# A chunked RWKV-7 scan: triangular inverse on 64 partitions, two 64-row product stages in one, and the scan's transfers merged and reordered

## The reference

```python
def step(state, inp):
    r_t, w_t, k_t, v_t, kk_t, a_t = inp
    sa = einsum('zbhvk,zbhk->zbhv', state, -kk_t)
    state = (state * w_t[..., None, :] + sa[..., :, None] * (kk_t * a_t)[..., None, :]
             + v_t[..., :, None] * k_t[..., None, :])
    y = einsum('zbhvk,zbhk->zbhv', state, r_t)
    return state, y
```

## Time and profile before

| | us |
|---|---|
| median of 3 runs (3359.9 to 3370.8) | 3364.0 |
| the profiled execution | 3362.9 |
| its span, first to last instruction | 3361.1 |

### The profile page before, as it was taken

One profiled execution on the slowest core, in us unless ns is written; L12 is line 12 of the kernel. 1 busy time (PEld: TensorE's weight loads), 2 busy tenths in 40 slices (PEclk: granted clock), 3 DMA queues, 4 the chain that ended last, 5 costly groups with the idle time before them and its releaser, 6 DMA issues.

```text
span 3361.1 us, 42103 instructions
## 1 busy us (share of the span) xinstructions
PE 3258.0 (97%) x15943; PEld 2692.0 (80%) x15943; DVE 1852.6 (55%) x2360; ACT 1310.0 (39%) x2139; POOL 1580.3 (47%) x1492
## 2 busy tenths in 40 slices
PE   7999999999889999999899999999999999999998
PEld 6788887777578888888588878888888888888886
DVE  3666565666667676772531034455455455455556
ACT  4544345554255665662442232223233233223222
POOL 4544443334278888885564443323323323323323
PEclk9999999999899999999899999999999999999999
DMA  5444454443455555552633323323323323323323
GB/s 171 122 151 138 141 154 132 129 120 103 114 137 143 129 130 141 146 135 82 242 115 136 113 69 113 107 88 107 112 83 109 111 81 117 103 84 117 107 82 106
DMA packets 666051, 405.06 MB, mean 121 GB/s; under 512 B 193534, under 2 KB 597178, under 8 KB 665338
## 3 DMA queue, kind: packets, MB, share of 16 engines
q1 hardware_dynamic: 665850, 402.38, 41.1%
HBM read 347.05 MB, written 54.53 MB: 119 GB/s over the span
## 4 chain that ended last, share of the span: by engine, by line
PE 50%; DVE 1%; ACT 0%; issue 0%; POOL 0%; DMA 0%; SPq 0%; DVEq 0%; ACTq 0%; POOLq 0%
PE f_bank L2207 9%; PE f_bank L2209 9%; PE f_bank L2208 9%; PE f_bank L2245 4%; PE f_bank L2247 4%; PE f_bank L2246 4%; PE f_bank L2185 2%; PE f_bank L2186 2%; PE f_bank L2187 2%; PE f_bank L2128 1%; PE f_bank L2129 1%; PE f_bank L2130 1%; PE f_bank L2163 0%; DMA orw_plain<-oat 0%; DVE orw_plain L2701 0%
## 5 line engine op out<-in xcount | busy, mean ns | idle before, releaser
L2496 POOL TENSOR_TENSOR w_lo_b<-w_raw_b,w_hi_b 128x1024 fp32r<-128x1024 f32 x176 | 435.9, 2479 | 903.4 <-ACT w_hi_b L2372 898.1
L2207 PE MATMUL f_bank<-act_rounded,w_lo_b 128*128 128x512 f32 x1408 | 549.2, 390 | 1.2 <-DVE act_rounded L2608 1.2
L2209 PE MATMUL f_bank<-act_rounded,w_hi_b 128*128 128x512 f32 x1408 | 547.8, 389 | 0.0
L2208 PE MATMUL f_bank<-act_rounded,w_hi_b 128*128 128x512 f32 x1408 | 547.8, 389 | 0.0
L1295 POOL TENSOR_TENSOR ring_w_rounded<-ring_w_plain,ring_w_hi 128x1024 fp32r<-128x1024 f32 x134 | 330.3, 2470 | 427.5 <-ACT ring_w_hi L1311 427.5
L1635 PE MATMUL slab_ps<-h_hi,ring_w_rounded 128*128 128x512 f32 x1056 | 426.4, 404 | 2.8 <-DVE h_lo L1462 2.4
L1636 PE MATMUL slab_ps<-h_lo,ring_w_hi 128*128 128x512 f32 x1056 | 414.9, 393 | 0.0
L1637 PE MATMUL slab_ps<-h_hi,ring_w_hi 128*128 128x512 f32 x1056 | 414.2, 392 | 0.0
L2372 ACT CAST w_hi_b<-w_raw_b 128x1024 fp32r<-128x1024 f32 x176 | 185.1, 1053 | 449.6 <-DMA w_raw_b<-in_w_ffn_up_dram 203.9
L2207 PEld LDWEIGHTS f_bank<-act_rounded,w_lo_b 128*128 128x128 f32 x1408 | 264.5, 188 | 55.7 <-DVE act_rounded L2608 1.1
L2209 PEld LDWEIGHTS f_bank<-act_rounded,w_hi_b 128*128 128x128 f32 x1408 | 264.3, 188 | 55.2
(11 more groups left out here) (434 smaller groups left out, 6176.9 us busy)
## 6 DMA issues: line engine op xcount, KB each, us to landing
ring_w_plain<-in_w_in_dram SPq DMA_DIRECT2D x190, 512.0 KB, 4.1
w_raw_b<-in_w_ffn_gate_dram SPq DMA_DIRECT2D x88, 512.0 KB, 3.6
w_raw_b<-in_w_ffn_up_dram SPq DMA_DIRECT2D x88, 512.0 KB, 3.6
w_raw_b<-in_w_ffn_down_dram SPq DMA_DIRECT2D x42, 512.0 KB, 3.9
w_raw_b<-in_w_out_dram SPq DMA_DIRECT2D x16, 1024.0 KB, 5.0
zt<-slab_out SPq DMA_DIRECT2D x63, 256.0 KB, 4.3
hid_plain<-in_w_ffn_down_dram SPq DMA_DIRECT2D x21, 512.0 KB, 4.2
oa_plain<-in_w_ffn_down_dram SPq DMA_DIRECT2D x21, 512.0 KB, 3.8
```

The costliest lines, as they stand in the source:

```text
L2207: pe.matmul(o, wl[:, k, :], act_hi[:, kk, :], start=kk == 0, stop=False)
L2208: pe.matmul(o, wh[:, k, :], act_lo[:, kk, :], start=False, stop=False)
L2209: return pe.matmul(o, wh[:, k, :], act_hi[:, kk, :], start=False, stop=stop)
L2496: pool.tensor_tensor(low(r), slab_raw(j % 2), high(r).bitcast(F32), ALU.subtract).then_inc(slab_low, 1)
```

## The change

- **Inverse (GpSimd).** Each matrix is now on two partitions, which hold the columns of one parity: 64 partitions with 32 matrices. 31 steps in place of 30, on at most 144 elements a partition in place of 240. The result is a tensor of its own, `inv`, cleared before each inverse; so the rows and columns of the matrices are put in an order of their own (even tokens first within a half, and for the backward direction the halves exchanged), which VectorE's masks (`mask_ba`, `mask_br`, `mask_ka`, made at the start) and the operands' order follow.
- **Products of b and k (TensorE).** The stages ab and ak become one, abk: 8 products of 64 rows, straight from `bk` and `var`, alternating between the two halves of the array's rows and between two banks. ScalarE's stage bd with its four copies goes. The masked results are taken by VectorE in three stages (n, ab, ak) with operations on 64 partitions, 8 in place of 5.
- **Transfers (SyncE).** The six loads of a unit become two, the five of the bonus two, since `zt` has its rows in another order. In odd slots the wait for the inverse, its store and the transfers into `d_bd` and `low` for one unit come before the loads of the next matrices; the other unit's transfers move to the start of the even slot.

```diff
-PE_SLOT = (("x1", "u"), ("ab", "v"), ("lx", "u"), ("ak", "v"), ("x3", "u"), ("av", "v"), ("qg", "u"),
+PE_SLOT = (("x1", "u"), ("abk", "v"), ("lx", "u"), ("x3", "u"), ("av", "v"), ("qg", "u"),
            ("bk", "v"), ("yh", "u"), ("akv", "v"), ("ts", "u"))
-GATE_SHARE = {"ab": 2, "ak": 2, "av": 3, "bk": 3, "akv": 3, "ts": 3}
-DVE_SLOT = (("ab", "v"), ("xadd", "u"), ("ak", "v"), ("decays", "w"), ("qg", "u"), ("operands", "w"), ("state", "u"))
+GATE_SHARE = {"abk": 2, "lx": 3, "av": 2, "bk": 3, "akv": 3, "ts": 3}
+DVE_SLOT = (("n", "v"), ("xadd", "u"), ("ab", "v"), ("ak", "v"), ("decays", "w"), ("qg", "u"), ("operands", "w"), ("state", "u"))
...
-                    for j in range(HALF - 2, 0, -1):
-                        n = HALF - 1 - j
-                        shape = [HALF, j, n]
-                        st = step[:, 0:j * n].rearrange("p (i t) -> p i t", t=n)
-                        pool.tensor_tensor(st, m[:, 0:j, j:j + 1].broadcast_to(shape), m[:, j:j + 1, j + 1:HALF].broadcast_to(shape),
-                                           ALU.mult).then_inc(inv_chain, 1)
+                    rows = lambda t: t.rearrange("p (r c) n -> p r c n", r=2)
+                    for j in range(HALF - 1, 0, -1):
+                        k, n, c, at = (j + 1) // 2, EVERY - j // 2, j // 2, (j % 2) * EVERY + j // 2
+                        shape = [CH, 2, k, n]
+                        st = step[:, 0:2 * k * n].rearrange("p (r i n) -> p r i n", r=2, n=n)
+                        pool.tensor_tensor(st, rows(m)[:, :, 0:k, at:at + 1].broadcast_to(shape),
+                                           x[:, at:at + 1, c:EVERY].unsqueeze(1).broadcast_to(shape), ALU.mult).then_inc(inv_chain, 1)
                         pool.wait_ge(inv_chain, done + 1)
-                        pool.tensor_tensor(m[:, 0:j, j + 1:HALF], m[:, 0:j, j + 1:HALF], st, ALU.add).then_inc(inv_chain, 1)
+                        pool.tensor_tensor(rows(x)[:, :, 0:k, c:EVERY], rows(x)[:, :, 0:k, c:EVERY], st, ALU.add).then_inc(inv_chain, 1)
...
+                    if slot % 2 == 0 and slot >= 0:
+                        blocks_back(slot + 1)
+                    paired = slot % 2 and 0 <= slot + 1 < NUNIT
+                    if paired:
+                        it = (slot + 1) // 2
+                        sp.wait_ge(inverted, it + 1)
+                        for r in range(2):
+                            sp.dma_start(yb[it % 2, :, :, r, :], inv[it % 2][r * HALF:(r + 1) * HALF, :, :]).then_inc(inv_stored[it % 2], 16)
                     if 0 <= v < NUNIT:
-                        it, s = divmod(v, 2)
-                        sp.wait_ge(taken_dve, DVE_AT["ab", v])
+                        sp.wait_ge(taken_dve, DVE_AT["n", v])
+                        sp.dma_start(nb[(v // 2) % 4, v % 2].rearrange("q p t -> p q t"), n_sb[:, :, :]).then_inc(n_stored, 16)
+                    if paired:
+                        sp.wait_ge(inv_stored[it % 2], 32 * (it // 2 + 1))
+                        blocks_back(slot + 1)
+                    if 0 <= v < NUNIT and v % 2:
+                        it = v // 2
+                        sp.wait_ge(n_stored, 16 * (v + 1))
+                        if it >= 2:
+                            sp.wait_ge(inverted, it - 1)
+                        src = nb[it % 4].rearrange("z q (e i) t -> (z q e) i t", e=2)
+                        for hb in range(2):
+                            for r in range(2):
+                                at = r * HALF + 16 * hb
+                                sp.dma_start(blocks[it % 2][at:at + 16, :, :],
+                                             src[:, hb * HALF:(hb + 1) * HALF, hb * HALF:(hb + 1) * HALF]).then_inc(n_landed[it % 2], 16)
...
-                    elif name == "ab":
-                        pe.wait_ge(taken_act, ACT_AT["bd", n])
+                    elif name == "abk":
+                        pe.wait_ge(taken_dve, DVE_AT["operands", n])
+                        if n >= 1:
+                            pe.wait_ge(taken_act, ACT_AT["akv", n - 1])
                         for q in Q:
-                            ins = pe.matmul(bank[1][:, q, :], b_bd[:, q, :], xar[st][:, q, CH:3 * CH], start=True, stop=True)
+                            for e in range(2):
+                                r = slice(CH * e, CH * e + CH)
+                                ins = pe.matmul(bank[1 + 2 * e][:, q, :], bk[r, q, :], var[r, q, CH:3 * CH], start=True, stop=True)
...
-                            dve.scalar_tensor_tensor(out=t[:, :, CH:P], in0=ordered(kk_in, s), scalar=-1.0, in1=by_scan(e_ex, s),
-                                                     op0=ALU.mult, op1=ALU.mult).then_inc(prep_ready, 1)
-                            dve.tensor_tensor(t[:, :, P:3 * CH], ordered(r_in, s), by_scan(e_in, s), ALU.mult)
...
-                            dve.tensor_copy(av[:, :, 0:CH], t[:, :, CH:P]).then_inc(taken_dve, 1)
+                            for r in range(2):
+                                dve.tensor_tensor(placed(var[:, :, CH:P], r), half(kk_in, back_in, r), half(e_ex, back_e, r), ALU.mult)
+                            dve.tensor_tensor(var[:, :, P:3 * CH], ordered(r_in, s), by_scan(e_in, s), ALU.mult)
+                            dve.tensor_tensor(xar[st][:, :, P:3 * CH], ordered(r_in, s), by_scan(e_in, s), ALU.mult)
```

More of the change, by code:

```diff
@@ L56 @@
 HALF = 32
+EVERY = HALF // 2
 PARAMS = {}
@@ L459, in store_gate, with blocks_back @@
                         sp.dma_start(zt[row:row + P, :], gate[c % 2][:, :]).then_inc(gate_stored[c % 2], 16)
-                def bonus_rows(b, row):
-                    return zt[row + (b // 2) * P:row + (b // 2 + 1) * P, (b % 2) * HS:(b % 2 + 1) * HS]
+                def blocks_back(n):
+                    it, s = divmod(n, 2)
+                    if n >= 2:
+                        sp.wait_ge(made, PE_AT["x3", n - 2])
+                    else:
+                        sp.wait_ge(zeroed, N_ZERO)
+                    for hb in range(2):
+                        first = 8 * (2 * hb + s)
+                        src = yb[it % 2].rearrange("b i r t -> b i (r t)")[first:first + 8].rearrange("(q e) i t -> e i q t", e=2)
+                        for e in range(2):
+                            at = CH * e + HALF * hb
+                            sp.dma_start(d_bd[s][at:at + HALF, :, at:at + HALF], src[e]).then_inc(d_landed[s], 16)
+                    for e in range(2):
+                        first, last = CH * e + HALF * s, CH * e + HALF * (1 - s)
+                        sp.dma_start(low[s][first:first + HALF, :, last:last + HALF],
+                                     nb[it % 4, s, :, first:first + HALF, last - CH * e:last - CH * e + HALF].rearrange("q i t -> i q t")
+                                     ).then_inc(d_landed[s], 16)
                 load(0)
@@ L643, in _, with in_turn @@
                 dve.wait_ge(zeroed, N_ZERO)
-                strict = g.order[:, 0:1, :].broadcast_to([P, NQ, CH])
-                within = g.order[:, 1:2, :].broadcast_to([P, NQ, CH])
+                each = lambda t: t[:, :].unsqueeze(1).broadcast_to([P, NQ, CH])
+                mask_ba, mask_br, mask_ka = ([each(t) for t in m] for m in masks)
+                mask_kr = each(g.order[:, 1, :])
+                tok = qg[:, 0:2, :].rearrange("p a n -> p (a n)")
+                dve.wait_ge(tokens_made, 3)
+                masks_done = [0]
+                def in_turn(ins, n=1):
+                    ins.then_inc(masks_made, 1)
+                    masks_done[0] += n
+                    dve.wait_ge(masks_made, masks_done[0])
+                row = [qg[:, 2, i:i + 1] for i in range(3)]
+                for i in range(3):
+                    in_turn(dve.tensor_tensor(qg[:, 3, 0:CH], tok[:, i * CH:(i + 1) * CH], g.eyes[:, :], ALU.mult))
+                    in_turn(dve.tensor_reduce(row[i], qg[:, 3, 0:CH], AX.X, ALU.add))
+                for i in range(2):
+                    place_a, natural = tok[:, i * CH:(i + 1) * CH], tok[:, 2 * CH:3 * CH]
+                    dve.tensor_scalar(masks[0][i][:, :], place_a, row[i], -1.0, ALU.is_gt, ALU.mult)
+                    dve.tensor_scalar(masks[1][i][:, :], natural, row[i], None, ALU.is_ge)
+                    in_turn(dve.tensor_scalar(masks[2][i][:, :], place_a, row[2], -1.0, ALU.is_gt, ALU.mult))
                 eyes = g.eyes[:, :].unsqueeze(1).broadcast_to([P, NQ, CH])
@@ L693, in _ @@
                         h = n // (2 * NCH)
[L694 to L695 removed]
+                        if name == "n":
+                            dve.wait_ge(made, PE_AT["abk", n])
                             if n >= 1:
                                 dve.wait_ge(n_stored, 16 * n)
[L698 to L699 removed]
+                            for e in range(2):
+                                r = slice(CH * e, CH * e + CH)
+                                ins = dve.tensor_tensor(n_sb[r, :, :], bank[1 + 2 * e][0:CH, :, 0:CH], mask_ba[s][0:CH], ALU.mult)
+                            ins.then_inc(taken_dve, 1)
```

(11 more changed lines are left out.)

169 lines of the change are left out of this document (72 added, 97 removed).

## The result

The changed kernel takes **3411.7 us** (median of 4 runs, 3406.8 to 3414.0), the kernel before, run beside it, 3362.0. The ratio is 1.0141, with a 95% interval from 1.0124 to 1.0158: slower by 1.4%. The forecast was 3366, from 3335 to 3396; the time lies outside. The profiled execution took 3410.2 us, its span is 3408.5.

What follows compares the result with a forecast made beforehand. The prediction took GpSimd (39.0 us a pair) and the matrix engine (38.0) as both near their limit; afterwards inverse plus turn, 39.6 us, would bind. With 3.0 + 0.7 = +3.7 on 3362.9 it said 3366 us, range 3335 to 3396.

Steps and rivals of the forecast that it cites:

- inverse: One GpSimd inverse, 62 dependent instructions on 64 partitions: 30.4 us, ends 28.5 and 33.5, against 39.0 before.
- turn: GpSimd's pause from one inverse's end to the next's start, through SyncE's stores, transfers and block loads: 9.2 us.
- The signs of being wrong: On GpSimd and TensorE: pauses under 8 us, an inverse above 32, or no wait at x1.
- fewer collisions with VectorE: In GpSimd's inverse: VectorE's two-input subtractions fall largely into GpSimd's idle quarter, so 1.5 us off.
- the second rival: GpSimd and SyncE: inverse or turn costs 1.6 us more, 41.2 us a pair, 3390 us; chance 0.24.
- serial loop clearly slower: GpSimd and SyncE: next blocks load only after the present inverse; 41.2 us a pair, 3390 us; chance 0.24.
- abk: TensorE's 8 half-height products replacing ab and ak: 1.2 us where 1.64 stood, 0.5 us a unit less.
- The rival of 0.06: On TensorE the half-height products don't pair: 0.5 us a unit lost, path 39.7, 3368 us; chance 0.06.
- TensorE's own path: The matrix engine's own time for a pair of units, without waiting for the inverse: 38.7 us.
- the wait at yh: TensorE waiting for qg at line 824, behind VectorE's longer list: 0.6 us even, 1.1 odd slots, 1.7 a pair.
- Masks, merged loads, ScalarE's four copies at nothing: VectorE's masks at the start and ScalarE's dropped copies: nothing; SyncE's merged loads pay for part of yh's wait.
- x1 after the inverse: Time from the last inverse's end on GpSimd to TensorE's product x1: 7.3 us, against 6.6 before.

Runs made afterwards that it cites:

- old kernel in the new order: Kernel before, only SyncE's odd slot reordered: inverse's wait, store and first unit's six transfers ahead of n_sb's store and next block loads; 3514.2 us.
- loads first: Changed kernel, SyncE's odd slot with n_sb's store and the four block loads ahead of the wait for the inverse, its stores and six transfers; 3324.5 us.

## Why the prediction was wrong

**The mechanism was right, two sizes were off, and they sat in a loop.** The prediction said: loop = inverse + turn = 30.4 + 9.2 = 39.6 us. It is 31.3 + 11.1 = 42.4. The 2.8 us come 15 times: 3366 + 42 = 3408 of 3411.7. Term by term, the last inverse ends at 1608.7 where 1564.1 was forecast, 44.6 us later: 29.1 of them are the 15 turns, 12.0 the 14 inverses in the middle, 2.3 the first inverse (34.3 for 32.0) and 1.1 its later start. The signs of being wrong that the prediction names hardly showed: every pause was over 8 us, x1 waited, and only the first inverse and two later ones, by up to 0.4, were above 32. They didn't ask whether a pause could be too long.

- *The turn, 9.2 taken, 11.1 measured: the step that failed.* Piece by piece (means of 15): d_bd's first transfer at T + 3.39, taken 2.8; six issues with gaps 2.75, taken 2.75; four block issues 1.96, taken 1.50; landing after them 2.81, taken 2.0; the rest, 0.2, is gaps. The inverse's stores had pieces of 64 bytes and the block loads twice as many pieces, and I gave them the old rows' durations, plus 0.4 for the pieces of the stores and nothing for those of the loads. The old kernel in the new order has the old pieces, and there the same terms are 2.06 to d_bd's first transfer (with one store), 1.5 and 2.1 us. The experiments take 1.0 us off the turn by one store of long runs and 1.5 by half the block loads. The Trainium skill (DMA: Bandwidth & Descriptors, "Specifications") asks for pieces of 512 B and more for full rate; the 2944 more packets under 512 B for each inverse agree with it as to the direction, while no run here varies the size alone.
- *The turn's range, 8.5 to 10.5, was too narrow*: 11.1 lies outside, and the prediction gives no reason for its upper end. With the inverse's own upper end of 33.5 the range should have reached 3366 + 15 x 4.4 = 3432.
- *The inverse, 30.4 taken, 31.3 measured*, inside 28.5 to 33.5. The interpolation's 31.5 was right; the 1.5 us for fewer collisions with VectorE were mostly not there. In loads first, VectorE busier, it takes 31.9, and in the changed kernel the last one takes 28.8, when the preparation of further units has ended. It is 2.4 us under the middle ones there, and before the last was 2.0 under them. With 60% of the elements and about as many instructions, the loss to VectorE has not shrunk; that fits the second rival's argument that it goes by instructions, though no run tests it alone.
- *The rival "serial loop clearly slower"* had its mechanism, but its price of 3390 rested on 41.2 us a pair, the inverse or the turn 1.6 us dearer, and it argued only for the inverse. Measured are both at once, 0.9 and 1.9. Its chance of 0.24 and a range end of 3396 followed from a turn taken as counted.
- *abk, 1.2 taken for 1.64*: 1.16 by its row, 1.09 from start to next start, 0.5 a slot. The length that recurs most among slots with 12 tiles and no wait is 18.50 us in loads first and 19.00 before. Right, as was the reason: unpaired it is 1.71 by its row and 1.64 from start to start. The rival of 0.06 is out. That the two halves of the array work side by side is what the Trainium skill (TensorEngine Tiling (Array Packing), "Key Properties") says, and the trace agrees: 1.16 against 1.71 us.
- *TensorE's own path, 38.7 taken, 36.7 measured in loads first.* The term most off is the wait at yh, 1.7 us a pair; it is 0.4, as before. I had let VectorE's 1.3 us through to yh nearly whole. Its wait for late inputs ahead of decays, which the prediction counted against a part of them, is gone (15.5 us in the 500 before, none listed in loads first); why the rest costs nothing wasn't traced. Of the other 0.7 us of the path, 0.2 are waits at yh that my 4.6 us left out, since the profile lists 2.5 more under two other names (7.1 in all); 0.5 stay open. Had I got this right and the turn as I did, the forecast would have been the same, for the loop bound.
- *Masks, merged loads, ScalarE's four copies at nothing*: for the loads it is shown (2 us, within the intervals); the others weren't tried by themselves.
- *x1 after the inverse, 7.3 us taken*: 7.4 (1108.93 less 1101.51).

The chances of .32 and .34 for faster and slower were those of someone who saw a loop and an open path 1 us apart. The error was to let the forecast rest on a difference of two terms of which one, the turn, was a sum of estimates for thirteen transfers.

## What to carry to other kernels

In a queue that serves in order, a wait for a long computation belongs behind the loads that the next such computation needs; here the same transfers in two orders give 3411.7 and 3324.5 us. Before shortening a stage, write down the loop that would then go round once per iteration, with the landing of each transfer in it, and allow for more pieces when a layout is split finer. And where a small wait is left at one place, move the cheapest operation that it may be waiting for, whatever name stands at the wait.

## What was not expected of the hardware

A TensorE that waits also comes back slower. In the changed kernel a slot after a long wait, beside one without, shows it (timeline of TensorE):

```profile
1084.66 1.05 PE L829 MATMUL sbank<-xar,d_bd 128*128 128x128 f32 x8
1085.64 1.16 PE L837 MATMUL sbank<-var,bk 64*128 64x128 f32 x16
...
1108.93 2.08 PE L829 MATMUL sbank<-xar,d_bd 128*128 128x128 f32 x8 [4.99 <-DMA low<-nb]
1110.94 1.75 PE L837 MATMUL sbank<-var,bk 64*128 64x128 f32 x16
```

After 4.99 us of waiting the same products took 2.08 and 1.75 us instead of 1.05 and 1.16. The granted clock is 0.50 of full speed in the 2.1 us from 1108.90, the lower of the two levels (1.2 instead of 2.4 GHz), 0.65 in the mean of the 1.7 us after them, and 1.00 from 1112.7 on. The mean granted clock of the 500 us falls with the pause before x1: 1.00 in loads first, 0.95 in the changed kernel, 0.91 in the old kernel with the new order, where x1 waits up to 9.6 us. x1 and abk are no part of the loop that GpSimd and the queue set, so I take it that this prolongs nothing here; what it costs was not tried.

GpSimd's additions and multiplies cost about the same on 64 partitions as on 32: multiply and add together 987 ns at 120 elements, where the line through the earlier trace rows at 108 and 150 gives 976. It differs by size: 611 ns for 530 at 30 elements, 1007 at 140 where the line gives 1104.
